# A two-layer transformer pair on one core: the first layer's feed-forward run once for both token streams, in two halves of its width

## What is computed

```python
h  = h  + mod[:, :, 2] * merge_branches(u, ...)          # likewise hc
u2 = modulate(rms_norm(h, g_norm2[l]), mod[:, :, 3], mod[:, :, 4])
h  = h  + mod[:, :, 5] * conv_ffn(u2, w_up[l], conv_w[l], conv_b[l], w_down[l])   # likewise hc, while l < DEPTH - 1

def conv_ffn(t, w_up, conv_w, conv_b, w_down):           # w_up 1024 x 5632, w_down 2816 x 1024
    a = dwconv(t @ w_up, conv_w, conv_b)                 # three taps along the tokens
    gate, val = jnp.split(a, 2, axis=-1)
    return (jax.nn.silu(gate) * val) @ w_down
```

## Time and profile before

| | us |
|---|---|
| median of 3 runs (lowest to highest) | 4173.27 (4172.57 to 4185.32) |
| the profiled execution | 4174.29 |
| its span, as the profile counts it | 4172.2 |
| PE busy / DVE busy / ACT busy | 3859.3 / 2307.8 / 1607.1 |

### The profile page before, as it was taken

One profiled execution on the slowest core, in us unless ns is written; L12 is line 12 of the kernel. 1 busy time (PEld: TensorE's weight loads), 2 busy tenths in 40 slices (PEclk: granted clock), 3 DMA queues, 4 the chain that ended last, 5 costly groups with the idle time before them and its releaser, 6 DMA issues. The chain is left out here.

```text
span 4172.2 us, 54081 instructions
## 1 busy us (share of the span) xinstructions
PE 3859.3 (93%) x20018; PEld 3033.7 (73%) x20018; DVE 2307.8 (55%) x3968; ACT 1607.1 (39%) x2718; POOL 310.3 (7%) x278
## 2 busy tenths in 40 slices
PE   5998989998999888999999899979899998989998
PEld 3875667777888787865678688856578886657886
DVE  6346577754553575365633556255657625566752
ACT  3235571112442453245632444233544424354431
POOL 0000001111000000110000100104010010400001
PEclk8999999999999999999999999989899999989999
DMA  5100005551222343200022222322023322202332
GB/s 178 60 28 19 1 27 178 187 193 56 96 96 101 103 160 119 78 29 19 1 91 86 81 96 96 100 66 73 26 86 96 101 90 83 81 21 86 95 103 78
DMA packets 86733, 350.90 MB, mean 84 GB/s; under 512 B 9520, under 2 KB 9648, under 8 KB 85680
## 3 DMA queue, kind: packets, MB, share of 16 engines
q1 hardware_dynamic: 72752, 298.53, 21.6%
q0 software_dynamic: 13824, 50.34, 3.6%
HBM read 346.73 MB, written 2.10 MB: 84 GB/s over the span
## 5 line engine op out<-in xcount | busy, mean ns | idle before, releaser
L503 DVE TENSOR_TENSOR split_low<-weight_ring,split_high 128x1024 fp32r<-128x1024 f32 (+2 forms) x460 | 623.1, 1355 | 668.7 <-ACT split_high L495 657.7
L495 ACT ACTIVATE split_high<-weight_ring 128x1024 fp32r<-128x1024 f32 (+2 forms) x474 | 535.0, 1130 | 892.0 <-PE banks L1475 469.6
L1631 PE MATMUL banks<-normed_high,split_high 128*128 128x512 f32 (+1 forms) x1760 | 654.3, 372 | 46.0 <-DVE normed_low L422 25.9
L1631 PE MATMUL banks<-normed_low,split_high 128*128 128x512 f32 (+1 forms) x1760 | 651.1, 370 | 0.0
L1631 PE MATMUL banks<-normed_high,split_low 128*128 128x512 f32 (+1 forms) x1760 | 650.9, 370 | 0.0
L1631 PEld LDWEIGHTS banks<-normed_high,split_high 128*128 128x128 f32 x1760 | 334.6, 190 | 109.4 <-issue 43.4
L1631 PEld LDWEIGHTS banks<-normed_high,split_low 128*128 128x128 f32 x1760 | 334.3, 190 | 56.0
L1631 PEld LDWEIGHTS banks<-normed_low,split_high 128*128 128x128 f32 x1760 | 334.6, 190 | 55.3
L1475 PE MATMUL banks<-hidden_high,split_high 128*128 128x512 f32 (+1 forms) x880 | 325.0, 369 | 9.5 <-DVE split_low L503 9.5
L1475 PE MATMUL banks<-hidden_low,split_high 128*128 128x512 f32 (+1 forms) x880 | 324.5, 369 | 0.0
L1475 PE MATMUL banks<-hidden_high,split_low 128*128 128x512 f32 (+1 forms) x880 | 324.2, 368 | 0.0
(11 more groups left out here) (327 smaller groups left out, 7211.7 us busy)
## 6 DMA issues: line engine op xcount, KB each, us to landing
weight_ring<-in_up SPq DMA_DIRECT2D x220, 512.0 KB, 3.5
weight_ring<-in_down SPq DMA_DIRECT2D x80, 704.0 KB, 4.0
modulation_ring<-in_ada POOLq DMA_DIRECT2D x80, 512.0 KB, 4.6
weight_ring<-in_merge SPq DMA_DIRECT2D x48, 768.0 KB, 4.3
weight_ring<-in_inputs SPq DMA_DIRECT2D x36, 512.0 KB, 3.5
weight_ring<-in_out SPq DMA_DIRECT2D x32, 512.0 KB, 3.5
latents<-in_ada POOLq DMA_DIRECT2D x16, 512.0 KB, 4.7
weight_ring<-in_xbc SPq DMA_DIRECT2D x16, 512.0 KB, 3.6
```

Source lines behind the costliest of these rows:

```text
L495: act.activation(k.splits[0][:, (n0 + panel) % RING, 0:width], k.slot(n0 + panel)[:, 0:width], ACT.Copy).then_inc(k.high_ready.sem, 1)
L503: dve.tensor_tensor(k.splits[1][:, s, 0:width], k.ring[:, s, 0:width], k.splits[0][:, s, 0:width].bitcast(F32), ALU.subtract).then_inc(k.l ...
L1631: last = pe.matmul(sums(r, half), w, x, start=(c + j == 0), stop=(c == KT - 1 and j == 2))
```

## The change

One function, `feed_forward_of_both`, takes the place of the two calls of `feed_forward` in layer 0. It norms both streams (`norm_streams`: all latent chunks, then all context chunks) and then runs `both_streams`: 11 tiles up, 8 output tiles down with the half of `w_down` that belongs to them, then the other 11 up and 8 down. Each panel is loaded and split once, and PE applies it to the 512 latent columns and then to the 256 context columns; `hidden` needs room for 11 tiles of 768 columns. The order of the panels in `lay_out` follows. The code of both phases is written out, where `ffn_up` and `add_product` loop on PE, DVE and SP. In the second phase the finished tiles are squared, added and summed for both streams, so layer 1's `project_inputs` squares nothing and takes its first panels' split later. `add_product` now squares all columns that it covers, both streams after the merge.

```diff
--- before.py
+++ after.py
...
+    squared = KT if l == 0 else 0
...
-            for n in range(KT):
+            for n in range(squared):
                 if n >= 2:
                     act.wait_ge(*k.squares_summed(n - 1))
                 act.activation(k.probs[:, n % 2, :], k.stream[:, n, :], ACT.Square).then_inc(k.squares_ready.sem, 1)
-            if not ada:
-                next_high(0)
-                next_high(1)
-            act.wait_ge(*k.squares_summed(KT))
+            if squared:
+                act.wait_ge(*k.squares_summed(KT))
             for s, (a, b) in enumerate(columns):
                 act.activation(k.probs[:, 2, a:b], k.psum[:, s, 0:b - a], ACT.Sqrt, bias=k.scalars[:, 12:13],
                                scale=1.0 / D).then_inc(k.deviation_ready.sem, 1)
-            if ada:
-                next_high(0)
-                next_high(1)
+            next_high(0)
+            next_high(1)
...
             if not ada:
-                next_low(0)
-                next_low(1)
                 invert()
             dve.wait_ge(*k.inverse_ready(2))
             dve.wait_ge(*k.gains_ready(1))
             scale_chunk(0)
-            if ada:
-                next_low(0)
+            next_low(0)
             for c in range(1, KT):
                 scale_chunk(c)
                 low_chunk(c - 1)
-                if ada and c == 2:
+                if c == 2:
                     next_low(1)
...
-    first, end = regions[0][0]
+    first, end = min(region[0][0] for region in regions), max(region[0][1] for region in regions)
     n = end - first
+    squared_columns = [(a - first, b - first) for (a, b), _, _ in regions]
...
-            pe.matmul(k.psum[:, SQUARES_BANK, 0:n], k.table("ones"), squared_tiles[:, 2, 0:n], start=True,
-                      stop=False)
+            for region, (a, b) in enumerate(squared_columns):
+                pe.matmul(k.psum[:, SQUARES_BANK + region, 0:b - a], k.table("ones"), squared_tiles[:, 2, a:b],
+                          start=True, stop=False)
             pe.wait_ge(*k.squares_ready(tiles))
-            pe.matmul(k.psum[:, SQUARES_BANK, 0:n], k.table("ones"), squared_tiles[:, (tiles - 1) % 2, 0:n],
-                      start=False, stop=True)
+            for region, (a, b) in enumerate(squared_columns):
+                pe.matmul(k.psum[:, SQUARES_BANK + region, 0:b - a], k.table("ones"),
+                          squared_tiles[:, (tiles - 1) % 2, a:b], start=False, stop=True)
...
-            act.wait_ge(*k.product_stored(R * squared + 1))
+            act.wait_ge(*k.product_stored(R * squared + R))
...
+def norm_streams(k, l, block, target, highs, lows, units):
...
+        for s, (a, b) in enumerate((LATC, CTXC)):
+            act.activation(k.probs[:, 2, a:b], k.psum[:, SQUARES_BANK + s, 0:b - a], ACT.Sqrt,
+                           bias=k.scalars[:, 12:13], scale=1.0 / D).then_inc(k.deviation_ready.sem, 1)
+        split_ahead(k, act, ahead)
+        for q, (c, s, a, b) in enumerate(units):
+            act.wait_ge(*k.scaled_ready(q + 1))
+            act.activation(highs[:, c, a:b], target[:, c, a:b], ACT.Identity, bias=shift(c, s)).then_inc(
+                k.high_ready.sem, 1)
...
+        modulated_gains(k, dve, l, 1)
+        for q, (c, s, a, b) in enumerate(units):
+            if c == 0:
+                dve.wait_ge(*k.deviation_ready(s + 1))
+                if s:
+                    low_part(q - 1)
+                dve.reciprocal(k.probs[:, 3, a:b], k.probs[:, 2, a:b]).then_inc(k.inverse_ready.sem, 1)
+                dve.wait_ge(*k.inverse_ready(s + 1))
+                dve.wait_ge(*k.gains_ready(1))
+            dve.scalar_tensor_tensor(target[:, c, a:b], k.stream[:, c, a:b], k.gains[:, 1, c, s:s + 1],
+                                     k.probs[:, 3, a:b], ALU.mult, ALU.mult).then_inc(k.scaled_ready.sem, 1)
+            if c:
+                low_part(q - 1)
+        low_part(len(units) - 1)
...
+HALF_TILES = FF_TILES // 2
+UP_JOBS = 2 * HALF_TILES
+PHASE_JOBS = UP_JOBS + KT
+def both_streams(k, l, block, highs, lows, hidden_highs, hidden_lows, weights, biases, scale):
...
+    def slot_of(f):
+        return f % HALF_TILES % 2
+    def sums(f, half, s):
+        a, b = streams[s]
+        return k.psum[:, 4 * s + 2 * slot_of(f) + half, 0:b - a]
+    def bank(t, s):
+        a, b = streams[s]
+        return k.psum[:, 4 * s + 2 + t % 2, 0:b - a]
...
+    @block.sync
+    def _(sp):
+        for j in range(total):
+            sp.wait_ge(*k.low_ready(j + 1))
+            k.load_panel(sp, n0 + j + RING)
+    @block.tensor
+    def _(pe):
...
+        def first_tile():
+            for c in range(KT):
+                pe.wait_ge(*k.normed_ready(c + 1 - 2 * KT))
+                for half in range(2):
+                    if c == 0:
+                        pe.wait_ge(*k.low_ready(half + 1))
+                    last = chunk(0, half, 0, c)
+                    if c == KT - 1:
+                        last.then_inc(k.product_ready.sem, 1)
+            for half in range(2):
+                for c in range(KT):
+                    if half == 0:
+                        pe.wait_ge(*k.normed_ready(c + 1 - KT))
+                    last = chunk(0, half, 1, c)
+                last.then_inc(k.product_ready.sem, 1)
+        def tile(f):
+            if f == HALF_TILES:
+                pe.wait_ge(*k.taps_added(8 * f))
+            elif f >= 2:
+                pe.wait_ge(*k.taps_added(8 * (f - 1)))
+            if f == HALF_TILES + 1:
+                pe.wait_ge(*k.product_stored(2 * KT))
+            for half in range(2):
+                pe.wait_ge(*k.low_ready(up_job(f, half) + 1))
+                for s in range(2):
+                    for c in range(KT):
+                        last = chunk(f, half, s, c)
+                    last.then_inc(k.product_ready.sem, 1)
+        def down(phase, t):
+            j = down_job(phase, t)
+            pe.wait_ge(*k.low_ready(j + 1))
+            if t == 0:
+                pe.wait_ge(*k.taps_added(8 * (HALF_TILES * (phase + 1) - 1)))
+                pe.wait_ge(*k.roped(HALF_TILES * (phase + 1) - 1))
+            elif t >= 2:
+                pe.wait_ge(*k.product_stored(2 * KT * phase + 2 * (t - 1)))
...
+        for m, start in ((2, True), ((KT - 1) % 2, False)):
+            pe.wait_ge(*(k.squares_added(KT - 2) if start else k.squares_ready(KT)))
+            for s, (a, b) in enumerate(streams):
+                pe.matmul(k.psum[:, s, 0:b - a], k.table("ones"), k.probs[:, m, a:b], start=start, stop=not start)
...
+        def next_high(j):
+            if j + 2 < total:
+                split_high(k, act, n0, j + 2, width(j + 2), None)
+        def centre(f, half, s):
+            a, b = streams[s]
+            at = half * FF_TILES + f
+            act.activation(buffer(f, half)[:, a:b], sums(f, half, s), ACT.Identity, bias=biases[:, at:at + 1],
+                           scale=weights[:, 1, at:at + 1]).then_inc(k.centre_ready.sem, 1)
+        def high_hidden(f):
+            act.wait_ge(*k.hidden_ready(f + 1))
+            act.activation(hidden_highs[:, f % HALF_TILES, :], buffer(f, 0), ACT.Copy).then_inc(
+                k.shifted_ready.sem, 1)
+        def tile(f):
+            for half in range(2):
+                for s in range(2):
+                    act.wait_ge(*k.product_ready(up_product(f, half, s)))
+                    if s:
+                        next_high(up_job(f, half))
+                    elif half == 0:
+                        act.wait_ge(*k.roped(f if f == HALF_TILES else f - 1))
+                    centre(f, half, s)
+                    if half + s == 0 and f % HALF_TILES:
+                        high_hidden(f - 1)
+                if half == 0:
+                    act.wait_ge(*k.taps_added(8 * f + 4))
+                    act.activation(buffer(f, 0), buffer(f, 0), ACT.Silu).then_inc(k.gated_ready.sem, 1)
+        def square(t):
+            act.wait_ge(*k.product_stored(2 * KT + 2 * t + 2))
+            if t >= 3:
+                act.wait_ge(*k.squares_added(t - 2))
+            act.activation(k.probs[:, t % 2 if t else 2, :], k.stream[:, t, :], ACT.Square).then_inc(
+                k.squares_ready.sem, 1)
+        for phase in range(2):
+            for f in range(HALF_TILES * phase, HALF_TILES * (phase + 1)):
+                tile(f)
+            high_hidden(HALF_TILES * (phase + 1) - 1)
+            for t in range(KT):
+                act.wait_ge(*k.product_ready(down_product(phase, t, 1)))
+                next_high(down_job(phase, t))
+                if phase and t:
+                    square(t - 1)
+        square(KT - 1)
+        act.activation(k.scalars[:, 15:16], k.scalars[:, 12:13], ACT.Sqrt)
...
+        def tile(f):
+            for half in range(2):
+                taps(f, half, 0)
+                if half == 0 and f % HALF_TILES:
+                    low_hidden(f - 1)
+                next_low(up_job(f, half))
+                taps(f, half, 1)
```

(25 more changed lines are left out.)

135 lines of the change are left out of this document (128 added, 7 removed).

## The result

The kernel after takes 4135.9 us (median of 4 runs, 4135.3 to 4136.66), the one before beside it 4179.17 (4172.57 to 4185.32): ratio 0.9897, 95% interval 0.9876 to 0.9917, faster by some 1%. A second set of runs gave 4134.9 and a ratio of 0.9907 [0.9891, 0.9924]. The forecast was 4131.5 with a range of 4124 to 4146. The profiled execution took 4135.3 for a span of 4133.5, 38.7 us less than the span before.

What follows compares the result with a forecast made beforehand. PE, busy 93% of the span, was taken as the bound, so only its idle time could give. Feed-forward 35.1 plus layer 1's norm 6.5 made 41.6 us saved: span 4130.6, time 4131.5 us, range 4124 to 4146.

Steps and rivals of the forecast that it cites:

- the feed-forward: Layer 0's merged feed-forward: 44 up jobs of 8.34 us, 16 down jobs of 11.47, ending 35.1 us earlier, at 1587.5.
- The first tile: Start of the feed-forward: low clock costs 2.8 us, before and after alike; late context chunks from DVE cost 1.3 us.
- the start: Feed-forward's first matmul comes 0.95 us later, through the longer last square, addition and sums; bounds 0.5 and 1.5.
- the gap: From last feed-forward matmul to layer 1's first product: 16.4 us against 22.94, 6.5 us saved.
- PE's sums, 2.8 us: In layer 1's norm, PE sums 512 + 256 columns twice: 2.8 us, with +2.8 as bound at half the clock.
- root to product: Layer 1's norm, square root to first product: 9.13 us before, 10.35 with a 1.22 us DVE subtraction added.
- The rest of the program keeps its lists: After layer 1's first product nothing changes, so the 41.6 us saved carry through to a span of 4130.6.
- PE waits for `split_low`, ACT for a panel from memory: Context's feed-forward before: PE waits 12 times for `split_low`, ACT 13 times for a panel, read as why it idles.
- The feeding of panels thin (1): Rival in the merged feed-forward: `split_low` late by some 0.3 us per job, 18 us, time 4150; chance 0.09.
- all 42 us gone to DVE (2): Rival: DVE's taps and splits, done again with 768 columns, cost 0.7 us per job, time 4173; chance 0.03.
- slow straight code (3): Rival: 3168 written-out matmuls in `both_streams` get instructions too slowly; 25 ns per matmul would make 4211; chance 0.02.
- a closer pitch (4): Rival: matmuls closer together, 7.80 us per job, over 46 us saved, time 4096; chance 0.01.

Runs made afterwards that it cites:

- the last experiment: Changed kernel with the early square and POOL doing layer 1's first subtraction, plus 18 unused PE matmuls in each of two gaps: 4134.14 us, ratio 0.9888.
- the early square: Changed kernel with ACT squaring tile t-1 before it waits for tile t's product in the second phase: 4132.1 us, ratio 0.9904.

## Why the prediction was right, point by point

**Right: the feed-forward.** 554.6 us were forecast and 554.71 measured; 8.34 us per up job exactly, 11.46 instead of 11.47 per down job, and 554.7 in all seven versions of it with another tail, load or delay. The first tile was forecast at 16.7 us of work, 2.8 of clock and 1.3 of waiting for context chunks, 20.8 in all, and took 20.91. The 1.3 was what the end of DVE's chunks (17.5 us after the first matmul, forecast and measured) left over behind the slow clock, so the DVE chain alone sets the tile's end: the last experiment, with no clock lost, takes the same. The split into clock and waiting has no meaning for the time, and the 2.8 us that the range kept for the clock there stand for a second loss, which didn't come.

**Right with an error in size: the start and the gap.** The norm ahead of the first matmul grew by 0.59 us (from the end of the merge product), not 0.95, and layer 0's attention happened to end 1.2 us earlier, which no part of the forecast had in it. In the gap, the term "PE's sums, 2.8 us" was mis-sized: 4.54, since the clock fell behind the 2.8 us in which PE waited for POOL (0.62 over the sums). The text had this as a bound (+2.8 at half the clock) and took the full clock; the eight sums without a pause take 3.01. POOL (1.80 for 1.9) and root to product (10.27 for 10.35) were as forecast. So the feed-forward ended 1.5 us earlier than forecast (1586.04 against 1587.5) and the gap was 1.5 us longer (17.89 against 16.4). That the two together made 41.66 for 41.6 is luck.

**Wrong: that nothing behind the gap moves.** "The rest of the program keeps its lists" carried 41.6 us to the end. At layer 1's first product it was 41.66. Then 1.4 and 1.6 us went, where the granted clock was lower than before (0.50 for 0.74, 0.80 for 0.90). These are the 2.9 us between the spans forecast and measured (4130.6, 4133.5). The other 1.5 of the 4.4 us between 4131.5 and 4135.9 come from the step from span to median, taken as 0.9 us and measured as 2.4. The section "What's actually happening" of the page "TensorE: Matmul & The Clock Gate" in the Trainium skill ties the clock to how busy PE was and says that the low stretch at the start varies with the run; the trace agrees for the first (0.50 behind a gap, 1.00 with PE kept busy). The second is about the start alone; the low stretches of layer 1 repeat within one kernel and differ between kernels.

**Wrong: the reading of the earlier trace rows.** "PE waits for `split_low`, ACT for a panel from memory" was taken for a shortage of transfers. Halving them gave 1 us; shortening the taps gave 11. What PE waited for was the chain of DVE's taps, silu, copy and subtraction, once in every second tile. The number was safe because the forecast did not depend on the cause, only on the new job having room: 8.34 us of PE over a chain of some 5 us.

**The rivals.** The feeding of panels thin (1), all 42 us gone to DVE (2) and slow straight code (3) are excluded by the job time of 8.34 us and an idle time of 0.56 of 540; a closer pitch (4) by the same row. The estimate of 7.80 us per job, from N / 2.4 GHz plus 2.5 ns in the section "Wait — 56ns, not 53.3ns?" of the Trainium skill's page "TensorE: Matmul & The Clock Gate", doesn't hold here.

## What to carry to other kernels

When PE waits for a product of ACT and DVE and one of these waits for a load, follow the queue behind each wait round to where it closes: the taps, the silu behind them and the copy behind the silu were to be seen in a dozen lines of timeline, and the wait for DMA beside them was filler. Then shorten one link and see how much comes back: here it was 11 us, about half of the 20 by which the taps of the 22 tiles were shortened. Serving more columns from each prepared panel is worth what that chain exceeds PE's work (18.6 us in the up tiles, whatever else is in it) plus one norm (14.0 us). The feed-forward itself could be forecast to 0.1 us from the time of one job and DVE's chain in the first tile; the total only to 4 us. A few microseconds saved at a pause may come back or not, depending on the clock in stages far behind: judge them at the edges of stages as well as by the total.

## What the runs showed of the hardware

- The time of an execution of one kernel goes with its mean granted clock. Of the 21 runs of the kernel before beside the experiments, one took 4168.89 us at 0.971, those at 0.969 4172.95 and 4173.41, those at 0.968 4173.27 to 4176.65, and those at 0.964 and 0.965 4182.16 to 4186.26. The version with the early square fell into 4126 to 4127 (0.970) and 4137 to 4138 (0.966 and 0.967).
- A kernel that came 1.3 us later to the feed-forward ended 4.1 later, one that came 1.1 later ended 3.1 later. Keeping PE busy over two gaps brought 2.2 us in the next stage; the same kernel lost 7.2 us in the first 111 us of layer 1's attention. What sets the clock in layer 1's attention stays open; its code is the same in all these kernels, so the difference comes from what went before it.
- The same 564 matmuls of layer 1's attention, with the work of ACT and DVE between them, take 98.05 us at a granted clock of 1.00, 99.65 at 0.98 and 103.63 at 0.93.
- POOL's addition of 768 columns takes 1.80 us with DVE idle and 2.54 at 1565.35, where a subtraction of DVE ran beside its first 0.9 us.
